# A pooling mixer and feed-forward trunk in split fp32: VectorE's transposes of three pairs of rows move within the second half's w_in products

## The chip, the cores and the metric

The kernel runs on one core of a Trainium2 chip. The metric is device time in microseconds (us): the median of three runs before the change is 1633.23 us (1632.07 to 1633.6).

The engines that matter here: TensorE (PE in the profile; PEld is its weight load), VectorE (DVE), ScalarE (ACT), GpSimd (POOL) and the queues from which transfers are issued (SPq, ACTq, and POOL's own).

## The reference, cut to what matters

Shapes: 2048 tokens of 1024 features, 16 meta tokens ahead of them, one layer (DEPTH is 1, so the mixer is the pooling one), d_ff is 2816.

```python
h = concatenate([meta, x])                       # 2064 x 1024
u = h @ a_w_in                                   # four groups of 256 columns
for g, w in enumerate((2, 4, 8, 16)):            # trailing mean over w tokens
    pooled[g] = (cs[hi, g] - cs[lo, g]) / (hi - lo)
y = einsum('btgc,gce->btge', pooled - u, a_w_group)
m = (y * a_scale) @ a_w_out
h = layer_norm(ALPHA * h + m, ln_mix_g, ln_mix_b)
gate, up = split(h @ ffn_w_gu, 2)
h = layer_norm(ALPHA * h + (silu(gate) * up) @ ffn_w_down, ln_ffn_g, ln_ffn_b)
return h[N_META:]
```

## The kernel before, in words

**Arithmetic.** Every fp32 operand of a product is split into a high part (a cast, on ScalarE, in functions that end in `_hi`) and a low part (original minus high, on VectorE, `_lo`). A product is then three matmuls of 128x512. The large products are done with seven block products instead of eight (sums and differences of quarter matrices, made on POOL and VectorE).

**Tiling.** The tokens are four blocks of 512 (b = 0 to 3), and two blocks are a half (h = 0, 1). For each half, `mixer_block(h)` computes u = x @ w_in in eight steps p, and `mixer_products(h)` the seven products with the folded group and output weights. The steps go through `STEPS = ((0,0), (0,1), (1,0), (1,1), (0,2), (0,3), (1,2), (1,3))`: block e of the half and chunk i of w_in, 256 columns. Step p is 48 matmuls on TensorE. The windows of the chunks are 16, 4, 8 and 2 (chunk 0 to 3). I call the eight steps of the second half p0 to p7.

**What a step brings with it.** When step p's matmuls are done, ScalarE copies them from PSUM to `stage` (`stage_u`, L1343). VectorE then pools them (`pool`, L1705 to L1720): copies of the 16 tokens of history, running sums (four, two, three or none), and a last subtraction into a `d` tile. TensorE has two PSUM places for the steps and takes the third step only when the first has been staged: step p waits for `stage_u` of step p-2. There is one `stage` tile, so `stage_u` of a step waits for the pooling of the step before it (`d_ready`). A chunk of w_in is used by two steps and is split anew in each half (`split_hi` L1308, `split_lo` L1672) into one of two places: the third chunk's split is needed by p4, the fourth's by p5. Its place comes free when p2, or p3, is done.

**The pairs.** During the second half's eight steps the normalised rows of the first half are transposed for the feed-forward product. They come back from DRAM in four pairs of row tiles, pi = 0 to 3. For each pair VectorE does four transposes (`turn_pair`, L1871), ScalarE scales and shifts them in eight instructions and issues their store (`scale_turned`, L1333 and L1323), and POOL makes four sums and issues their store (`pair_sums`, L987, L936, L994). The tiles of pairs 0 and 2 are `st_mix0`, those of pairs 1 and 3 `st_mix1`. The memory of `st_mix0` is also the tile `d12`, into which p4 and p5 are pooled. So the pooling of p4 in the second half waits for the store of pair 2 to land (`st_stored[0]` at 32) and for POOL's sums of pairs 0 to 2 (`ss_made` at 12). POOL's sums of a pair wait for its scaling; the transposes of pair 2 or 3 wait for the store of the pair that held the tile, and for its sums.

**Order.** Each engine runs its own instructions in the order in which the functions for it are written; nothing reorders them. The sync queue's order is written out too; its loads of the next x rows (`load_z`) wait for the number of transposes done (`turn_done`).

Of the kernel before, what the change touches and what calls it, by code (L numbers as in the profile page):

```python
# [31 lines left out]
def trunk(nc, x, x_t, meta_t, w_in, first_t, second_t, w_group_t, w_out, mix_g, mix_b, w_gu, w_down, ffn_g, ffn_b,  # L32
# [7 lines left out]
    TT = TOK // P  # L40
# [22 lines left out]
    def c_in(h, i):  # L63
        return MIX0 + h * HALF_CHUNKS + i
# [10 lines left out]
    def used_up(c):  # L75

        h, r = (c - MIX0) // HALF_CHUNKS, (c - MIX0) % HALF_CHUNKS
        return c + 1 if c < MIX0 else in_done(2 * h + 1, r) if r < PAIRS else mix_done(h, r - PAIRS)
# [13 lines left out]
    with ExitStack() as ctx:  # L92
# [256 lines left out]
        def raw_of(c, slot):  # L349
            return raw_first[:] if c == c_in(0, 0) else raw[:, slot]  # L350
# [58 lines left out]
        def st_of(pi):  # L409
            return st_mix[pi % 2] if pi < 4 else st_gu  # L410
# [893 lines left out]
        def _(act):  # L1304
            def split_hi(c, slot, kn=CHUNK):
                act.wait_ge(raw_landed[slot], (c - slot) * 8 - 8 * (GROUPS - 2))
                act.wait_ge(chunk_done, used_up(c - 2))
                nc.scalar.copy(split[:, slot, 0, 0:kn], raw_of(c, slot)[:, 0:kn]).then_inc(w_hi_ready, 1)  # L1308
# [12 lines left out]
            def store_turned(pi):  # L1321
                act.wait_ge(turn_taken, 2 * TT * (pi + 1))
                nc.scalar.dma_start(pair_forms(pi)[:, 0:3, :], st_of(pi)[:, 1:4].rearrange("p f k t -> p f (k t)")  # L1323
                                    ).then_inc(st_stored[pi % 2], 16)

            def scale_turned(pi, kh):

                act.wait_ge(turn_done, TT * pi + 3 + kh)
                if pi == 0:
                    act.wait_ge(mix_gb_kept, 1)  # L1330
                for k in range(KC):
                    both, kk = st_of(pi)[:, 2 * kh:2 * kh + 2, k, :], kh * KC + k
                    nc.scalar.activation(both, both, ACT.Identity, bias=mix_b_sb[:, kk:kk + 1],  # L1333
                                         scale=mix_g_sb[:, kk:kk + 1]).then_inc(turn_taken, 1)
                if kh:
                    store_turned(pi)

            def stage_u(b, i):
                act.wait_ge(chunk_done, in_done(b, i))
                if b or i:  # L1340

                    act.wait_ge(d_ready, staged_by(b, i) - 1)
                nc.scalar.mul(staged(), pair(i % 2), 1.0 / WINDOWS[ORDER[i]]).then_inc(u_staged, 1)  # L1343

            def d_hi(h, t):
                form_ready(act, h, t)

                act.wait_ge(chunk_done, in_done(2 * h, PAIRS - 1) if t < 2 else mix_done(h, t - 2))
                nc.scalar.copy(ring[h][t % 2][:, 0], FORM_D[t][:]).then_inc(d_hi_ready, 1)
# [58 lines left out]
            def stage_meta(i):  # L1408
                act.wait_ge(meta_rows_done, i + 1)
                if i >= 1:  # L1410
                    act.wait_ge(meta_u_done, i)
                nc.scalar.mul(meta_rows[:], acc[:, 4, 0:CW], 1.0 / WINDOWS[ORDER[i]]
                              ).then_inc(meta_rows_staged, 1)
# [43 lines left out]
            def norm(s, j):  # L1457
                act.wait_ge(shift_ready, s + 1)
                zz = zm[s % 2][:, j, :]
                nc.scalar.activation(zz, zz, ACT.Identity, bias=shift[:, j:j + 1],  # L1460
                                     scale=rstd[:, j:j + 1]).then_inc(normed, 1)

            def mixer_block(h):
                for p, (e, i) in enumerate(STEPS):
                    b = 2 * h + e
                    c = c_in(h, 0) + {0: 1, 3: 2, 4: 3, 7: 4}.get(p, 0)
                    if c > c_in(h, 0) and c != c_in(0, 1):
                        split_hi(c, c % 2)
                    if p >= 1:
                        stage_u(2 * h + STEPS[p - 1][0], STEPS[p - 1][1])  # L1470
                    if b == 0:
                        stage_meta(i)
                    if h and 2 <= p <= TT + 1:
                        scale_turned(p - 2, 0)
                        scale_turned(p - 2, 1)
                    if p >= 6:
                        d_hi(h, p - 6)
                    if p < 2:
                        x_hi(2 * h + 1, 2 * p)
                        x_hi(2 * h + 1, 2 * p + 1)  # L1480
                    if h and p == 0:
                        for j in range(TT):
                            norm(1, j)
# [185 lines left out]
        def _(dve):  # L1669
# [190 lines left out]
            def turn_pair(pi):  # L1860
                if pi < 2:

                    dve.wait_ge(d_lo_ready, NP)
                else:
                    dve.wait_ge(st_stored[pi % 2], 16 * (pi // 2))
                    dve.wait_ge(ss_made, 4 * (pi - 1))
                for step, n in enumerate(TURN_ORDER):
                    if step % 2 == 0:
                        dve.wait_ge(z_landed[1 - step // 2][pi], 16 + 16 * QT)
                    dst, src = turned_block(pi, n)  # L1870
                    nc.vector.transpose(dst, src).then_inc(turn_done, 1)  # L1871

            def mixer_block(h):
                for p, (e, i) in enumerate(STEPS):
                    c = c_in(h, 0) + {0: 1, 3: 2, 4: 3, 7: 4}.get(p, 0)
                    if c > c_in(h, 0) and c != c_in(0, 1):
                        split_lo(c, c % 2)
                    if p == 7:
                        d_sums(h, 0)
                        d_sums(h, 1)  # L1880
                    if h and p == 0:
                        rows_stats(0, 6)
                        stats_are_done(1)
                        aggregate(1)
                    if p < 2:
                        x_lo(2 * h + 1, 2 * p)
                        x_lo(2 * h + 1, 2 * p + 1)
                    if h == 0 and p in (1, 2, 5, 6):
                        taken = (1, 2, 5, 6).index(p)
                        take_meta(taken)  # L1890
                        dve.wait_ge(meta_u_taken, taken + 1)
                    if h == 0 and p == 1:
                        for n in range(2):
                            dve.wait_ge(fold_stored[n], 16 * GROUPS)
                    if h and p in (4, 5):
                        turn_pair(p - 2)
                    if p >= 1:
                        pool(2 * h + STEPS[p - 1][0], STEPS[p - 1][1])
                    if h and p in (1, 2):
                        turn_pair(p - 1)  # L1900
                    if p == 6:
                        d_lo(h, 0)

# [355 lines left out]
```

## Time and profile before

| What | Value |
|---|---|
| Median of the runs | 1633.23 us |
| Profiled execution, its own time | 1632.91 us |
| Its span (first to last instruction) | 1631.1 us |
| Granted TensorE clock over the span | 1.00 |
| PE busy | 1620.8 us, 99% |
| DVE, ACT, POOL busy | 65%, 37%, 39% |
| Transfers | 326.63 MB, 200 GB/s in the mean |

How to read it. An engine's busy time is a mean over stages that differ much. PE is busy almost throughout, so a change can matter only where it shortens or adds a wait of PE, and such waits are read one by one from the timeline. In a timeline row the first number is the start, the second the length of the group, and the bracket holds the idle time before it with what ended it. The releaser is inferred from semaphores.

### The profile page before, as it was taken

How to read it: one execution, taken by the hardware profiler on the slowest of the kernel's cores; microseconds unless marked ns; L12 is line 12 of the kernel's file. 1: busy time of each engine (PE TensorE's matmuls, PEld its weight loads, DVE VectorE, ACT ScalarE, POOL GpSimd, SP SyncE). 2: the span in 40 equal slices, each digit the busy share in tenths (PEclk: the TensorE clock that was granted, in tenths of full speed). 3: DMA queues.
4: the chain of work that ended last, by engine and by line, in shares of the span. 5: the costliest groups of instructions: out<-in, count | busy, mean ns of one | idle time of the engine just before them, and what ended most of it. 6: DMA issues, size and time to landing. Idle time of an engine off the chain costs nothing.

```text
span 1631.1 us, 18826 instructions
## 1 busy us (share of the span) xinstructions
PE 1620.8 (99%) x7169; PEld 1340.4 (82%) x7169; DVE 1052.5 (65%) x1111; ACT 608.1 (37%) x837; POOL 635.9 (39%) x440
## 2 busy tenths in 40 slices
PE   9999999999999999999999999999999999999998
PEld 7888887888888888888888888888888888888886
DVE  7758779998355556545756776676544443468866
ACT  6225454545434443434433333333333322222230
POOL 0420025025358667754456666666620000441000
PEclk9999999999999999999999999999999999999999
DMA  9563588444467666666856666665577544554542
GB/s 366 204 249 138 183 223 291 180 177 143 140 215 238 202 197 205 203 204 219 265 184 196 194 207 212 212 195 181 185 247 247 190 153 143 201 210 176 200 140 95
DMA packets 197001, 326.63 MB, mean 200 GB/s; under 512 B 8752, under 2 KB 140976, under 8 KB 188208
## 3 DMA queue, kind: packets, MB, share of 16 engines
q1 hardware_dynamic: 157216, 293.45, 53.9%
q10 hardware_dynamic: 37520, 23.60, 4.7%
q0 software_dynamic: 2176, 8.39, 1.4%
q8 instruction: 57, 0.93, 0.2%
q14 instruction: 32, 0.26, 0.0%
HBM read 223.16 MB, written 102.24 MB: 199 GB/s over the span
## 4 chain that ended last, share of the span: by engine, by line
PE 95%; DVE 2%; DMA 2%; issue 0%; ACT 0%; POOL 0%; SPq 0%; DVEq 0%; ACTq 0%
PE acc L1257 43%; PE acc L1287 19%; PE acc L1104 7%; PE turn L1257 7%; PE acc L1135 7%; PE turn L1287 6%; PE turn L1135 3%; PE acc L1167 1%; DVE sums L1717 1%; DMA dwr<-w_down 1%; DVE st_mix L1871 1%; DMA h_dram<-zm 1%; PE acc L1180 0%; DMA zm<-h_dram 0%; DVE split L1672 0%
## 5 line engine op out<-in xcount | busy, mean ns | idle before, releaser
L1257 PE MATMUL acc<-fa,wf 128*128 128x512 f32 x1584 | 362.8, 389 | 0.0
L1257 PE MATMUL acc<-fb,wf 128*128 128x512 f32 x1584 | 362.8, 389 | 0.0
L1257 PEld LDWEIGHTS acc<-fa,wf 128*128 128x128 f32 x1584 | 297.2, 188 | 61.8
L1257 PEld LDWEIGHTS acc<-fb,wf 128*128 128x128 f32 x1584 | 297.2, 188 | 61.8 <-issue 0.2
L1287 PE MATMUL acc<-dw,da 128*128 128x512 f32 x1386 | 315.6, 389 | 0.3 <-DVE dw L1972 0.3
L1287 PEld LDWEIGHTS acc<-dw,da 128*128 128x128 f32 x1386 | 260.1, 188 | 54.7 <-DVE dw L1972 0.7
L1857 DVE TENSOR_TENSOR wf<-wt,wf 128x512 fp32r<-128x512 f32 x132 | 130.1, 988 | 144.0 <-ACT wf L1454 144.0
L1857 DVE TENSOR_TENSOR wf<-wr,wf 128x512 fp32r<-128x512 f32 x176 | 181.8, 1039 | 38.8 <-ACT wf L1454 38.4
L936 POOL TENSOR_TENSOR wt<-wr,wt 128x512 f32<-128x512 f32 x88 | 138.7, 1577 | 154.6 <-DVE wf L1857 154.5
L1454 ACT CAST wf<-wr 128x512 fp32r<-128x512 f32 x176 | 108.7, 618 | 215.9 <-PE acc L1257 213.2
L1104 PE MATMUL acc<-mov,split 128*128 128x512 f32 x768 | 176.2, 390 | 1.8 <-DVE split L1672 1.8
L1966 DVE TENSOR_TENSOR da<-dar,da 128x1408 fp32r<-128x1408 f32 x56 | 92.1, 1644 | 132.0 <-ACT da L1555 132.0
L1104 PEld LDWEIGHTS acc<-mov,split 128*128 128x128 f32 x768 | 143.6, 188 | 32.2 <-issue 2.6
L1555 ACT CAST da<-dar 128x1408 fp32r<-128x1408 f32 x56 | 76.9, 1373 | 197.0 <-PE acc L1287 156.6
L1135 PE MATMUL acc<-split,ring 128*128 128x512 f32 x480 | 110.4, 389 | 0.0
L1287 PE MATMUL turn<-dw,da 128*128 128x512 f32 x462 | 105.9, 389 | 0.0
L1135 PEld LDWEIGHTS acc<-split,ring 128*128 128x128 f32 x480 | 90.1, 188 | 18.7
L1454 ACT CAST wf<-wt 128x512 fp32r<-128x512 f32 x132 | 81.9, 621 | 56.5 <-PE acc L1257 41.6
L1287 PEld LDWEIGHTS turn<-dw,da 128*128 128x128 f32 x462 | 86.7, 188 | 18.0
L936 POOL TENSOR_TENSOR wt<-wr 128x512 f32<-128x512 f32 x44 | 59.6, 1355 | 103.2 <-DMA wr<-w_gu 73.2
L1079 POOL TENSOR_TENSOR z<-z,z 128x512 f32<-128x512 f32 x8 | 12.2, 1526 | 199.1 <-DVE z L2106 199.1
L1972 DVE TENSOR_TENSOR dw<-dwr,dw 128x512 fp32r<-128x512 f32 x77 | 54.4, 732 | 41.5 <-ACT dw L1561 41.4
(151 smaller groups left out, 1810.8 us busy)
## 6 DMA issues: line engine op xcount, KB each, us to landing
wr<-w_gu SPq DMA_DIRECT2D x44, 1024.0 KB, 5.2
dar<-af_dram SPq DMA_DIRECT2D x56, 704.0 KB, 4.4
af_dram<-g ACTq DMA_DIRECT2D x32, 512.0 KB, 5.5
fs<-hf_dram SPq DMA_DIRECT2D x14, 1024.0 KB, 5.6
dt_raw<-w_down SPq DMA_DIRECT2D x22, 512.0 KB, 5.5
wt_dram<-dt_t SPq DMA_DIRECT2D x22, 512.0 KB, 3.5
sa<-af_dram SPq DMA_DIRECT2D x22, 512.0 KB, 8.2
af_dram<-sx SPq DMA_DIRECT2D x22, 512.0 KB, 4.7
```

Of the source, the lines that this page charges most:

```text
L936: return nc.gpsimd.tensor_tensor(out_, a, b, ALU.subtract)
L1104: mm = nc.tensor.matmul(acc[:, 2 * banks + m, :], w[:, a, k, m * P:(m + 1) * P], x_of[:, k, v, :], start=k == 0 and n3 == 0, stop=k == KT ...
L1135: mm = nc.tensor.matmul(bank_, ring[h][t % 2][:, v, k, m * P:(m + 1) * P], w[:, a, k, :], start=t in (0, 3) and k == 0 and n3 == 0, stop=k ...
L1167: mm = nc.tensor.matmul(acc[:, 2 * (q % 3) + n, :], gt[:, a, e, ct * P:(ct + 1) * P], w[:, v, e, n * TOK:(n + 1) * TOK], start=e == 0 and ...
L1257: mm = nc.tensor.matmul(dst, wf[:, slot, a, k, :], fa[half][i][:, v, :, k, :], start=i < 2 and k == 0 and n3 == 0, stop=k == KC - 1 and n3 ...
L1287: mm = nc.tensor.matmul(down_bank(k), da[k % 3][:, v, p, :], dw[:, slot, a, :], start=t < NP - 1 and p == 0 and n3 == 0, stop=p == JF - 1 ...
L1454: nc.scalar.copy(wf[:, (NP * n + i) % 8, 0].rearrange("p k n -> p (k n)"), w_source(n, i)).then_inc(wf_hi, 1)
L1555: nc.scalar.copy(da[k % 3][:, 0], dar[:, k % 2]).then_inc(da_hi, 1)
L1717: linked(nc.vector.tensor_tensor(nxt[:, :, lo:], cur[:, :, lo:], cur[:, :, lo - shift:H + TOK - shift], ALU.add))
L1857: nc.vector.tensor_tensor(wf[:, s, 1].rearrange("p k n -> p (k n)"), w_source(n, i), f32(wf[:, s, 0]).rearrange("p k n -> p (k n)"), ALU.s ...
L1966: nc.vector.tensor_tensor(da[k % 3][:, 1], dar[:, k % 2], f32(da[k % 3][:, 0]), ALU.subtract).then_inc(da_lo, 1)
L1972: nc.vector.tensor_tensor(dw[:, v % 16, 1, :], dwr[:, w % 2, v % JF % 2, :], f32(dw[:, v % 16, 0, :]), ALU.subtract).then_inc(dw_lo, 1)
```

## The change: three pairs' transposes take other places

The transposes, scalings and stores themselves are the same, and so is every wait. What moves, in the second half only:

- On VectorE the second pair (pi = 1) goes from behind p1's pooling, ahead of the third chunk's split, to behind the fourth chunk's split. The third pair (pi = 2) goes from there to a place behind p3's pooling, and is followed by the fourth (pi = 3), which stood there already.
- On ScalarE the first pair's scaling goes from ahead of the third chunk's cast to behind it, the second pair's from behind the staging of p2 to behind that of p3, and the third's from there to behind the staging of p4, ahead of the fourth pair's.

```diff
 # ScalarE, mixer_block(h), step p
                     if c > c_in(h, 0) and c != c_in(0, 1):
                         split_hi(c, c % 2)
+                    if h and p == 3:
+                        scale_turned(0, 0)
+                        scale_turned(0, 1)
                     if p >= 1:
                         stage_u(2 * h + STEPS[p - 1][0], STEPS[p - 1][1])
                     if b == 0:
                         stage_meta(i)
-                    if h and 2 <= p <= TT + 1:
-                        scale_turned(p - 2, 0)
-                        scale_turned(p - 2, 1)
+                    for pi in {4: (1,), 5: (2, 3)}.get(p, ()) if h else ():
+                        scale_turned(pi, 0)
+                        scale_turned(pi, 1)
 # VectorE, mixer_block(h), step p
-                    if h and p in (4, 5):
-                        turn_pair(p - 2)
+                    for pi in {4: (1,), 5: (2, 3)}.get(p, ()) if h else ():
+                        turn_pair(pi)
                     if p >= 1:
                         pool(2 * h + STEPS[p - 1][0], STEPS[p - 1][1])
-                    if h and p in (1, 2):
-                        turn_pair(p - 1)
+                    if h and p == 1:
+                        turn_pair(0)
```

On VectorE before, from the end of p1's pooling to the fourth chunk's split (`st_mix1_82` is the second pair's tile, `zm0`, `zm1` the rows that came back, `split` the two splits of w_in's third and fourth chunk, and between them stands p2's pooling with its four `sums`):

```order
L1720 SCALAR_TENSOR_TENSOR d0_60<-stage_73,sums0_68 128x1024
L1871 STREAM_TRANSPOSE st_mix1_82<-zm1_78 128x4x4x32 x2
L1871 STREAM_TRANSPOSE st_mix1_82<-zm0_77 128x4x4x32 x2
L1672 TENSOR_TENSOR split_70<-raw_71,split_70 128x2048
L1705 COPY stage_73<-hist_74 128x2x16
L1706 COPY hist_74<-stage_73 128x32
L1717 TENSOR_TENSOR sums1_69<-stage_73 128x2x526
L1717 TENSOR_TENSOR sums0_68<-sums1_69 128x2x524
L1717 TENSOR_TENSOR sums1_69<-sums0_68 128x2x520
L1717 TENSOR_TENSOR sums0_68<-sums1_69 128x2x512
L1720 SCALAR_TENSOR_TENSOR d1_61<-stage_73,sums0_68 128x1024
L1672 TENSOR_TENSOR split_70<-raw_71,split_70 128x2048
```

The same stretch of VectorE now (line numbers are three higher):

```order
L1723 SCALAR_TENSOR_TENSOR d0_60<-stage_73,sums0_68 128x1024
L1675 TENSOR_TENSOR split_70<-raw_71,split_70 128x2048
L1708 COPY stage_73<-hist_74 128x2x16
L1709 COPY hist_74<-stage_73 128x32
L1720 TENSOR_TENSOR sums1_69<-stage_73 128x2x526
L1720 TENSOR_TENSOR sums0_68<-sums1_69 128x2x524
L1720 TENSOR_TENSOR sums1_69<-sums0_68 128x2x520
L1720 TENSOR_TENSOR sums0_68<-sums1_69 128x2x512
L1723 SCALAR_TENSOR_TENSOR d1_61<-stage_73,sums0_68 128x1024
L1675 TENSOR_TENSOR split_70<-raw_71,split_70 128x2048
L1874 STREAM_TRANSPOSE st_mix1_82<-zm1_78 128x4x4x32 x2
L1874 STREAM_TRANSPOSE st_mix1_82<-zm0_77 128x4x4x32 x2
```

The second pair's transposes moved from ahead of the third chunk's split to behind the fourth's, past p2's pooling.

On VectorE before, what follows, up to the first copy of p4's pooling (`st_mix0_81` is the third pair's tile, `st_mix1_82` now the fourth's, and the pooling between them is p3's):

```order
L1871 STREAM_TRANSPOSE st_mix0_81<-zm1_78 128x4x4x32 x2
L1871 STREAM_TRANSPOSE st_mix0_81<-zm0_77 128x4x4x32 x2
L1705 COPY stage_73<-hist_74 128x2x16
L1706 COPY hist_74<-stage_73 128x32
L1717 TENSOR_TENSOR sums1_69<-stage_73 128x2x514
L1717 TENSOR_TENSOR sums0_68<-sums1_69 128x2x512
L1720 SCALAR_TENSOR_TENSOR d1_61<-stage_73,sums0_68 128x1024
L1871 STREAM_TRANSPOSE st_mix1_82<-zm1_78 128x4x4x32 x2
L1871 STREAM_TRANSPOSE st_mix1_82<-zm0_77 128x4x4x32 x2
L1705 COPY stage_73<-hist_74 128x2x16
```

And now, behind the second pair:

```order
L1708 COPY stage_73<-hist_74 128x2x16
L1709 COPY hist_74<-stage_73 128x32
L1720 TENSOR_TENSOR sums1_69<-stage_73 128x2x514
L1720 TENSOR_TENSOR sums0_68<-sums1_69 128x2x512
L1723 SCALAR_TENSOR_TENSOR d1_61<-stage_73,sums0_68 128x1024
L1874 STREAM_TRANSPOSE st_mix0_81<-zm1_78 128x4x4x32 x2
L1874 STREAM_TRANSPOSE st_mix0_81<-zm0_77 128x4x4x32 x2
L1874 STREAM_TRANSPOSE st_mix1_82<-zm1_78 128x4x4x32 x2
L1874 STREAM_TRANSPOSE st_mix1_82<-zm0_77 128x4x4x32 x2
L1708 COPY stage_73<-hist_74 128x2x16
```

The third pair moved behind p3's pooling and stands directly ahead of the fourth, and both ahead of p4's pooling.

On ScalarE before, from the staging of p1 to that of p4 (`split` is the cast of the third and of the fourth chunk, the `ACTIVATE` rows with x8 the scaling of the first, second and third pair, `hf_dram` their stores):

```order
L1343 ACTIVATE stage_73<-acc 128x2x512
L1333 ACTIVATE st_mix0_81<-st_mix0_81,mix_gb_sb 128x2x128 x8
L1323 DMA hf_dram<-st_mix0_81 128x3x512
L1308 CAST split_70<-raw_71 128x2048
L1343 ACTIVATE stage_73<-acc 128x2x512
L1333 ACTIVATE st_mix1_82<-st_mix1_82,mix_gb_sb 128x2x128 x8
L1323 DMA hf_dram<-st_mix1_82 128x3x512
L1308 CAST split_70<-raw_71 128x2048
L1343 ACTIVATE stage_73<-acc 128x2x512
L1333 ACTIVATE st_mix0_81<-st_mix0_81,mix_gb_sb 128x2x128 x8
L1323 DMA hf_dram<-st_mix0_81 128x3x512
L1343 ACTIVATE stage_73<-acc 128x2x512
```

And now:

```order
L1343 ACTIVATE stage_73<-acc 128x2x512
L1308 CAST split_70<-raw_71 128x2048
L1333 ACTIVATE st_mix0_81<-st_mix0_81,mix_gb_sb 128x2x128 x8
L1323 DMA hf_dram<-st_mix0_81 128x3x512
L1343 ACTIVATE stage_73<-acc 128x2x512
L1308 CAST split_70<-raw_71 128x2048
L1343 ACTIVATE stage_73<-acc 128x2x512
L1333 ACTIVATE st_mix1_82<-st_mix1_82,mix_gb_sb 128x2x128 x8
L1323 DMA hf_dram<-st_mix1_82 128x3x512
L1343 ACTIVATE stage_73<-acc 128x2x512
L1333 ACTIVATE st_mix0_81<-st_mix0_81,mix_gb_sb 128x2x128 x8
L1323 DMA hf_dram<-st_mix0_81 128x3x512
```

The cast of each chunk stands ahead of a scaling that it stood behind, the staging of p2 stays behind the first pair's, and those of p3 and p4 come ahead of the second and the third pair's. The fourth pair's scaling follows the third's.

## Rows read from the trace of the kernel before

**Rows 1.** The page's head: span, and busy time of TensorE.

```profile
span 1631.1 us, 18826 instructions
PE 1620.8 (99%) x7169; PEld 1340.4 (82%) x7169; DVE 1052.5 (65%) x1111; ACT 608.1 (37%) x837; POOL 635.9 (39%) x440
```

**Rows 2.** Timeline of TensorE around the second half's w_in steps.

```profile
201.62 43.68 PE L1104 MATMUL acc<-mov,split 128*128 128x512 f32 x192
245.46 11.16 PE L1104 MATMUL acc<-mov,split 128*128 128x512 f32 x48 [0.16 <-DVE split L1672]
258.26 32.95 PE L1104 MATMUL acc<-mov,split 128*128 128x512 f32 x144 [1.64 <-DVE split L1672]
291.05 5.60 PE L1135 MATMUL acc<-split,ring 128*128 128x512 f32 x24
```

**Rows 3.** Chain that ended last, by time: start, us, what.

```profile
255.83 2.30 DVE split L1672
...
291.21 5.44 PE acc L1135 x24
```

**Rows 4.** Timeline of VectorE, p0's pooling to p5's.

```profile
220.59 0.17 DVE L1705 COPY stage<-hist 128x32 f32<-128x32 f32 x1
...
222.18 3.79 DVE L1717 TENSOR_TENSOR sums<-sums 128x1048 f32<-128x1048 f32 x3
226.00 1.23 DVE L1720 SCALAR_TENSOR_TENSOR d<-stage,sums 128x1024 f32<-128x1024 f32 x1
...
238.03 4.37 DVE L1871 STREAM_TRANSPOSE st_mix<-zm 128x512 f32<-128x512 f32 x4
242.34 2.98 DVE L1672 TENSOR_TENSOR split<-raw,split 128x2048 fp32r<-128x2048 f32 x1
245.24 0.17 DVE L1705 COPY stage<-hist 128x32 f32<-128x32 f32 x1
...
247.95 6.70 DVE L1717 TENSOR_TENSOR sums<-sums 128x1048 f32<-128x1048 f32 x3
...
258.03 4.36 DVE L1871 STREAM_TRANSPOSE st_mix<-zm 128x512 f32<-128x512 f32 x4
262.30 0.15 DVE L1705 COPY stage<-hist 128x32 f32<-128x32 f32 x1
...
266.23 4.35 DVE L1871 STREAM_TRANSPOSE st_mix<-zm 128x512 f32<-128x512 f32 x4
271.49 0.18 DVE L1705 COPY stage<-hist 128x32 f32<-128x32 f32 x1 [0.91 <-POOL ss_mix L936]
...
276.57 2.19 DVE L1720 SCALAR_TENSOR_TENSOR d<-stage,sums 128x1024 f32<-128x1024 f32 x1
```

**Rows 5.** Timeline of ScalarE: a chunk's cast, the third pair's scaling, p5's staging.

```profile
237.74 1.92 ACT L1308 CAST split<-raw 128x2048 fp32r<-128x2048 f32 x1 [0.51 <-ACT st_mix L1333]
...
261.37 4.06 ACT L1333 ACTIVATE st_mix<-st_mix,mix_gb_sb 128x256 f32<-128x256 f32 x8 [4.33 <-DVE st_mix L1871]
...
278.86 1.03 ACT L1343 ACTIVATE stage<-acc 128x1024 f32<-128x1024 f32 x1 [5.25 <-DVE d L1720]
```

**Rows 6.** Timeline of POOL: the first of the third pair's four sums.

```profile
265.51 1.97 POOL L987 TENSOR_TENSOR ss_mix<-st_mix 128x512 f32<-128x512 f32 x1 [10.75 <-ACT st_mix L1333]
```

**Rows 7.** View of tile st_mix, 264 to 268 us: the third pair's store.

```profile
DMA to landing us min/median/max: 5.3/5.3/5.3
```

**Rows 8.** View of tile st_mix, 272 to 277 us: the fourth pair's store.

```profile
DMA to landing us min/median/max: 11.8/11.8/11.8
```

**Rows 9.** DMA view, 279 to 282 us: packets, MB, share (q0 POOL's, q1 SP's, q10 ACT's).

```profile
q0 software_dynamic: 128, 0.52, 42.4%
q1 hardware_dynamic: 129, 0.46, 37.7%
q10 hardware_dynamic: 128, 0.26, 22.4%
```

**Rows 10.** Timeline of TensorE at the program's start.

```profile
1.32 3.94 PE L1143 MATMUL turn<-idle 128*128 128x512 f32 x9 [1.32 <-POOL idle L1035]
```

## The prediction, on record before the result

> **What bounds the kernel now.** I read the page's head first: TensorE is busy for 99% of the span [rows 1], so only what lengthens or shortens a wait of TensorE can move the time. Next I read TensorE's timeline over the second half's eight w_in steps, p0 to p7, where the moved work lies [rows 2]. A group of 24 matmuls at full pace takes 5.44 us [rows 3], so a step of 48 takes 10.88. From p0's start at 201.62 the free grid of starts is p4 245.14, p5 256.02, p6 266.90, p7 277.78 and the end 288.66. The trace has p4 at 245.46 and p5 at 258.26, each released by VectorE's split of a w_in chunk, and the next stage at 291.05 [rows 2]. Of the 2.39 us behind the grid, 0.32 fall before p4, another 1.92 before p5 (1.64 shown as idle) and 0.15 after it. Counted back from 291.05, p7 started at 280.17. The chain of waits runs over VectorE's split at 255.83 [rows 3] and, from p5 on, over TensorE alone.
>
> VectorE's timeline says why the split was late: it is full [rows 4]. The transposes of the second pair (4.37 us at 238.03) stand ahead of the third chunk's split, and p2's pooling runs from 245.24 to 255.83, 10.6 us, where p0's with the same instructions takes 6.6 (220.59 to 227.23). Its sums beside POOL's take about 2.2 us each (6.70 for three) against 1.26 (3.79 for three).
>
> One more wait has almost no room. `stage_u` of p5 ran from 278.86 to 279.89 [rows 5], 0.28 us ahead of p7, which needs it. It stood behind p4's pooling, which began at 271.49 and ended at 278.76, and this began when POOL's sums of the third pair were done [rows 4]. The moved work acts on exactly this chain.
>
> **Part by part: what comes earlier.** The third chunk's cast no longer stands behind a scaling. It starts when p2 is done (201.62 + 3 x 10.88, about 234.4) and ends at 236.3. The first pair's scaling follows (4.06 us, the third pair's row [rows 5]) to 240.4, its store is issued, and p2's staging (1.03) ends at 242.0. VectorE splits the third chunk behind p1's pooling, from 238.0 to 240.3 (2.29, without the collision that made it 2.98 [rows 3, 4]), so p4 starts on the grid. Then VectorE idles for 1.7 us, as p2 isn't staged before 242.0. POOL's sums of the first pair now start at 240.5, and three of the four run beside p2's pooling. I charge each with the 1.0 us that the rows show: 6.6 + 3.0, ending at 251.5. The fourth chunk's split ends at 253.8, and p5 can start on the grid, at 256.02. Both waits on splits go: 2.24 us.
>
> **What comes later.** Behind that split come the second pair's transposes (4.3 us, to 258.1), then p3's pooling (4.0, as from 262.30 to 266.23 [rows 4], now to 262.0), and only then the third pair's. They start at 262.0 instead of 258.03, 4 us later although everything ahead of them was earlier: a pooling of 4.0 us was put in front, 1.7 us of idle was added, and less contention gave some back. Scaling ends 7.4 us after the transposes start (258.03 to 265.43 [rows 4, 5]), so at 269.4, and there the store is issued. POOL's four sums were done 13.3 us after the start (at 271.4, as p4's pooling shows [rows 4]); their first one took 1.97 beside VectorE's sums [rows 6], and is now free (1.3 like the others), so 12.7 and 274.7.
>
> p4's pooling waits for both the sums and the landing of this store. Before, the store landed 5.3 us after issue [rows 7], just inside the sums. Now it has company: the second pair's sums end on POOL at about 267, and their 1 MB store follows at once; the fourth pair's transposes (from 267.1, when the second pair's sums free the tile, to 271.4) release five loads of rows. The fourth pair's store of before lay in just such company and took 11.8 us [rows 8]. I take the middle of 5.3 and 11.8, 8.6 us, and land at 278.0. The bounds are 274.7 and 281.2.
>
> The rows show how the queues share: in 3 us with all three at work each moved 128 or 129 packets, and ScalarE's, with the smallest ones, 0.26 MB of them [rows 9]. The Trainium skill (DMA: Bandwidth & Descriptors, Queues, rings and completion order) says that each engine takes turns between the queues by packets, and the trace agrees. By that rule alone, with the 0.79 MB (128 x 3 x 512 words) at 0.087 MB per us throughout, the landing would take 9.1 us; with the first part beside one other queue it comes to about my 8.6.
>
> p4's pooling took 7.3 us beside POOL's sums of the fourth pair [rows 4]. It meets them again (POOL waits for its own second-pair store, which lands in the same crowd), so 278.1 + 7.3 = 285.4. Bounds: 5.3 without POOL (two sums and the end at their free 1.26 instead of 2.2), 8.3 if all four long instructions meet it. Staging p5 adds 0.1 + 1.03: 286.6. p7 starts there instead of 280.17. **Term one: +6.4 us**, in which the 2.24 gained are already used up, because p7 waits for staging and not for p6.
>
> **The clock behind the wait.** TensorE then idles from 277.78 to 286.6, 8.8 us. This trace has no such idle in its middle: the granted clock stands at 1.00 (the 2.4 GHz level) everywhere. The nearest row is the program's start: behind the pause before it, nine matmuls of the same 128x512 shape take 3.94 us, 0.438 each [rows 10], against 0.227 at full pace, although the clock column says 1.00 there too. That is the pace of the lower level. If the pause at p7 does the same, nine matmuls cost 9 x 0.211 = 1.9 us. Bounds: 0, and 3.2 if it is 15 matmuls. **Term two: +1.9 us**. The Trainium skill (TensorE: Matmul & The Clock Gate, Part 1) says that TensorE falls to 1.2 GHz when idle and regains 2.4 GHz only after activity; by it term two is in the sum, by the clock column of the start it isn't.
>
> **What costs nothing.** Transposes, scalings, sums and stores keep their number and size. The sync queue's loads of the next rows wait for transposes: two of them and a chunk load behind them come about 4 us later (the chunk is cast only after p6), the other five about 0.8. The fourth pair's scaling, now behind the third's, ends at about 274.5, while p4's pooling is held anyway. Behind p5's staging VectorE's work moves with TensorE's, both by 7 to 8 us, so the room between them stays. The end is untouched.
>
> **Sum.** 1632.91 (the profiled execution) + 6.4 + 1.9 = 1641.2. The median of the runs is 0.3 above that execution, so 1641.5.
>
> **Rivals.**
> - Late landing, but the clock holds: 1641.5 - 1.9 = 1639.6. For it: the clock column of rows 10 never leaves 1.00. Against it: the pace there.
> - The store lands inside the sums. Then p4's pooling starts at 274.8 and p7 at 274.8 + 7.3 + 1.1 = 283.2: +3.0, with the clock term 1638.1, without it 1636.2; if it also misses POOL's sums, +1.0 and 1634.2. For it: 5.3 us last time. Against it: 1 MB more in flight.
> - Not slower: VectorE's relief is all that counts. The two split waits go, p7 starts at 277.78, and the time is 1633.2 - 2.4 = 1630.8. It decides where p5 is staged by 277.8, so p4's pooling must start by 277.8 - 1.1 - 5.3 = 271.4, earlier than before; even a tie needs a start by 273.8. The third pair's transposes would have to start at 258.7 (for 271.4 behind 12.7), 3.3 us ahead of my 262.0. For it: VectorE does gain before p5. Against it: no row among the six in front can shrink by that.
> - Worse in two places: p2's pooling meets all of POOL's sums and more, the fourth chunk's split misses 256.02 as well, and all later terms grow; with the upper bounds 290.7 for p7, +10.5 + 3.2, 1646.9.
>
> That the change does nothing is out: the order of both engines moves as shown.
>
> **How the numbers follow.** Late landing with the lower clock 0.45 (1641.5), late landing without it 0.23 (1639.6), landing inside the sums with the clock term 0.12 (1638.1), the same without it 0.09 (1634.2 to 1636.2), relief alone 0.04 (1630.8), worse 0.07 (up to 1646.9). About 0.2%, 3.3 us, is what can be told from no change, so slower means above 1636.5: 0.45 + 0.23 + 0.12 + 0.07 = 0.87. Relief alone gives 2.4 us, which is within that bound too; I keep 0.01 of its 0.04 for more. So within is 0.09 + 0.03 = 0.12 and faster 0.01. The range 1635.5 to 1645.0 leaves out the case of relief, part of the within case and the worst end.
>
> **What would show it.** Right: no wait of TensorE on a split at p4 and p5; VectorE idle for 1 to 2 us ahead of p2's pooling; the third pair's transposes at about 262; p4's pooling released at 275 to 281 by the third pair's store or sums; one wait of TensorE of 6 to 10 us for p5's staging; slower matmuls right behind it. Wrong: p7 at or before 280.2, the third pair's transposes before 259, a PE wait on a split that stays, or waits in the mixer's products that were not there.

## The result, and the profile after

| | Before | After |
|---|---|---|
| Median, us | 1633.19 (1632.07 to 1633.6) | 1646.51 (1646.1 to 1646.95) |
| Ratio to before | | 1.0084 (95% interval 1.0071 to 1.0096) |
| Span of the profiled execution, us | 1631.1 | 1645.0 |
| Mean granted clock | 1.00 | 0.994 |

The change makes the kernel 13.3 us slower. The forecast was slower, at 1641.5 us with a range up to 1645.0; the measured time lies above the range.

TensorE's timeline after, where [rows 2] stand for before:

```profile
201.47 76.32 PE L1104 MATMUL acc<-mov,split 128*128 128x512 f32 x336
291.77 13.94 PE L1104 MATMUL acc<-mov,split 128*128 128x512 f32 x48 [13.97 <-ACT stage L1343]
305.55 5.60 PE L1135 MATMUL acc<-split,ring 128*128 128x512 f32 x24
```

The 336 matmuls are p0 to p6 in one piece: both waits on splits are gone. Then comes one wait of 14 us, for `stage_u` of p5, and p7 takes 13.8 us (291.77 to 305.55) instead of 10.9. Counted from p0's start, p7 comes 11.75 us later than before (90.30 against 280.17 - 201.62 = 78.55), and its slow pace adds 2.90. Those 14.65 us, less 0.15 by which p0 itself starts earlier and 0.6 by which the stretch from p7's end to the span's end is shorter, are the 13.9 between the spans.

VectorE's timeline after; the first row is the second pair's transposes, the next two are the third's and the fourth's, and the rest is p4's pooling:

```profile
253.60 4.27 DVE L1874 STREAM_TRANSPOSE st_mix<-zm 128x512 f32<-128x512 f32 x4
...
261.72 4.32 DVE L1874 STREAM_TRANSPOSE st_mix<-zm 128x512 f32<-128x512 f32 x4
266.94 4.32 DVE L1874 STREAM_TRANSPOSE st_mix<-zm 128x512 f32<-128x512 f32 x4 [0.90 <-issue]
282.48 1.90 DVE L1708 COPY stage<-hist 128x32 f32<-128x32 f32 x1 [11.22 <-DMA hf_dram<-st_mix]
284.41 0.18 DVE L1709 COPY hist<-stage 128x32 f32<-128x32 f32 x1
284.51 2.30 DVE L1720 TENSOR_TENSOR sums<-stage 128x1036 f32<-128x1036 f32 x1
...
289.37 1.23 DVE L1723 SCALAR_TENSOR_TENSOR d<-stage,sums 128x1024 f32<-128x1024 f32 x1
```

The third pair starts at 261.72 (forecast 262.0). p4's pooling starts at 282.48 (forecast 278.1), released by a transfer, and takes 8.1 us (forecast 7.3). Its first copy, of 32 elements in a row, takes 1.90 us against 0.18 before.

The chain of waits after names the transfer (start, us, what):

```profile
265.03 4.07 ACT st_mix L1333 x8
269.10 0.02 issue
269.12 13.28 DMA hf_dram<-st_mix
...
290.69 1.03 ACT stage L1343
291.72 0.04 issue
291.77 13.94 PE acc L1104 x48
```

The third pair's store takes 13.28 us, where it took 5.3 [rows 7]. The clock fell behind the wait; columns are the stretch, its length, PE busy, granted clock, share and rate of the transfers:

```profile
280.00:284.00 4.00, 0.00 (x0) 0.58 1.04 418
284.00:291.00 7.00, 0.00 (x0) 0.50 0.55 222
292.00:296.00 4.00, 4.00 (x10) 0.50 0.63 240
296.00:298.00 2.00, 2.00 (x6) 0.58 0.00 0
298.00:300.00 2.00, 2.00 (x10) 1.00 0.43 78
```

From about 281 to 297.5 us the granted clock is 0.50, the 1.2 GHz level.

### The profile page after: what moved, and what is told of

It reads as the page before. It is cut to its first block, busy times and chain, and to the rows that moved or that the text cites. A ratio compares the mean times of both kernels' runs of the same rounds, so it can differ in the third digit from the quotient of the medians.

```text
span 1645.0 us, 18826 instructions
## 1 busy us (share of the span) xinstructions
PE 1622.6 (99%) x7169; PEld 1342.6 (82%) x7169; DVE 1053.7 (64%) x1111; ACT 607.9 (37%) x837; POOL 630.5 (38%) x440
## 4 chain that ended last, share of the span: by engine, by line
PE 96%; DVE 2%; DMA 1%; ACT 1%; issue 0%; POOL 0%; DVEq 0%; ACTq 0%; SPq 0%
PE acc L1257 44%; PE acc L1287 19%; PE acc L1104 8%; PE turn L1257 7%; PE acc L1135 7%; PE turn L1287 6%; PE turn L1135 3%; PE acc L1167 1%; DMA hf_dram<-st_mix 1%; ACT st_mix L1333 1%; DVE sums L1720 1%; PE acc L1180 0%; DVE st_mix L1874 0%; DMA raw<-w_out 0%; DVE stage L1708 0%
```

## The experiments

Theory: the time went into the third pair, transposed later, whose store p4's pooling waits for, and into the lower clock behind that wait. Which transfers made the store late, and what made the pooling long, was open after the first four runs. The runs were made on three chips, so each is set against before on its own chip.

| Run | Median, us | Before on the same chip | Ratio, 95% interval |
|---|---|---|---|
| e1_third_back | 1638.14 (1635.57 to 1639.94) | 1632.51 | 1.0034 (1.0022 to 1.0045) |
| e2_second_back | 1641.69 | 1632.51 | 1.0058 (1.0043 to 1.0073) |
| e3_fill | 1644.66 | 1632.51 | 1.0075 (1.0058 to 1.0092) |
| e4_second_mid | 1634.33 | 1632.51 | 1.0011 (1.0002 to 1.0021) |
| e5_rows_late | 1646.03 | 1632.91 | 1.0080 (1.0065 to 1.0095) |
| e6_sums_store_late | 1638.24 | 1632.91 | 1.0033 (1.0021 to 1.0045) |
| e7_after_hold | 1643.25 | 1632.91 | 1.0062 (1.0045 to 1.0079) |
| e8_second_back_hold | 1634.85 | 1632.91 | 1.0011 (1.0002 to 1.0020) |
| e9_mid_hold | 1630.22 | 1632.85 | 0.9985 (0.9976 to 0.9994) |
| e10_before_hold | 1630.90 | 1632.85 | 0.9988 (0.9979 to 0.9997) |

### One part undone: the third pair back ahead of p3's pooling (e1)

The edit against the changed kernel, the same on ScalarE and VectorE (cut to the part that differs):

```diff
-{4: (1,), 5: (2, 3)}
+{4: (1, 2), 5: (3,)}
```

> The changed kernel with one part undone: the third pair stands again ahead of p3's pooling, now directly behind the second pair; the fourth alone in front of p4's pooling. Theory (the time went into the late third pair, whose store p4's pooling waits for, and into the lower clock behind that wait): transposes of the third pair start at 258, its store is issued at about 265.6 with only a chunk load beside it and lands in 5 to 6 us, POOL's sums of it end at about 273 behind those of the second pair; p7 starts at 280 to 282.5, a wait of TensorE of 2 to 5 us, 1633 to 1638 us. Rival A (the second pair's late place is what costs): the time stays at 1645 or more. Rival B (it is the number of transposes in a row ahead of a pooling that costs, wherever they stand): a wait of TensorE for p3's pooling appears at p6, and the time is above 1638.

1638.14 us, just above the theory's range, and the reason is another: rival B's. TensorE's timeline:

```profile
254.71 12.18 PE L1104 MATMUL acc<-mov,split 128*128 128x512 f32 x53
270.31 23.85 PE L1104 MATMUL acc<-mov,split 128*128 128x512 f32 x96 [3.42 <-ACT stage L1343]
```

The wait stands ahead of p6, not p7. p3's pooling behind two pairs of transposes ran from 262.0 to 269.1 beside POOL's sums, 7.1 us instead of 4.0, so p4 was staged late. The third pair's store landed in 6.7 us, as the theory said, and was not the bound. The clock fell behind this wait too (0.60 from 270 to 272 us, 0.54 from 272 to 274): p6 and p7 take 23.7 us (270.31 to 294.00) instead of 21.8. Wait and clock together are 5.3 of the 5.6 us above before. Putting the third pair back wins 8 of the 13 us, but directly behind the second pair it makes p6 late.

### The other part undone: the second pair back (e2)

The edit on VectorE, against the changed kernel. On ScalarE the scalings of the first and of the second pair go back to where they were before.

```diff
-                    for pi in {4: (1,), 5: (2, 3)}.get(p, ()) if h else ():
+                    for pi in {5: (2, 3)}.get(p, ()) if h else ():
                         turn_pair(pi)
...
-                    if h and p == 1:
-                        turn_pair(0)
+                    if h and p in (1, 2):
+                        turn_pair(p - 1)
```

> The other part undone: the second pair is transposed and scaled where it was before the change (behind p1's pooling), only the third pair moves behind p3's pooling, ahead of the fourth. Theory: the wait on the split at p5 comes back (1.6 us), the third pair's transposes start at about 262.2, its store shares the queues with the five row loads but not with a store of the second pair's sums, and lands 8 to 11 us after its issue at 269.6; p7 starts at 286 to 289 instead of 280.2, the clock falls to 0.5 behind the wait and costs 2.9 us more: 1641 to 1645 us. Rival A (the second pair's move, by its sums' store in flight, is what made the store late): the landing takes 5 to 6 us, p4's pooling waits for the sums, p7 at 283, 1636 to 1639 us. Rival C (the third pair's place costs nothing by itself): 1633 us.

1641.69 us, inside the theory's range, but not by its mechanism. The store landed in 5.7 us, as rival A expected, although the five row loads were in flight (issued from 270.43 on, the store at 269.24):

```profile
DMA to landing us min/median/max: 5.7/5.7/5.7
```

VectorE's timeline shows where the time went instead:

```profile
274.99 4.51 DVE L1705 COPY stage<-hist 128x32 f32<-128x32 f32 x1 [4.63 <-DMA hf_dram<-st_mix]
279.52 0.18 DVE L1706 COPY hist<-stage 128x32 f32<-128x32 f32 x1
279.62 2.32 DVE L1717 TENSOR_TENSOR sums<-stage 128x1036 f32<-128x1036 f32 x1
```

A copy of 128x32 took 4.51 us. With it p4's pooling took 10.7 us, and TensorE waited 6.7 us ahead of p7. POOL's rows beside it, the fourth pair's sums:

```profile
274.87 0.78 POOL L994 DMA_DIRECT2D hf_dram<-ss_mix  x1 [0.40 <-POOL ss_mix L936]
275.66 1.30 POOL L987 TENSOR_TENSOR ss_mix<-st_mix 128x512 f32<-128x512 f32 x1
276.91 1.29 POOL L936 TENSOR_TENSOR ss_mix<-st_mix 128x512 f32<-128x512 f32 x1
278.16 1.28 POOL L936 TENSOR_TENSOR ss_mix<-ss_mix,st_mix 128x512 f32<-128x512 f32 x1
279.52 1.32 POOL L936 TENSOR_TENSOR ss_mix<-st_mix,ss_mix 128x512 f32<-128x512 f32 x1
```

POOL runs at its free pace of 1.3 us each, and the copy ends in the gap between its third and fourth instruction. This run gave two new suspects: the store of the second pair's sums, for the landing, and POOL's instructions, for the pooling.

### Matmuls in the wait (e3)

```diff
+            FILL = 56
...
+                    if h and p == 7:
+                        chunk_is_split(c_in(h, i))
+                        wx = split[:, c_in(h, i) % 2].rearrange("p s (k n) -> p s k n", n=CW)
+                        for _ in range(FILL):
+                            nc.tensor.matmul(turn[:, 1, :], wx[:, 0, 0, 0:P], mov_of(b)[:, 0, 0, :], start=True, stop=True)
                     if p >= 2:
                         pe.wait_ge(u_staged, 2 * PAIRS * h + p - 1)
```

> The changed kernel with 56 more matmuls of 128x512 on TensorE between p6 and the wait of p7; they write a PSUM place that nothing reads, and take 12.7 us of the 14 us wait. Theory (the clock fell because TensorE was idle): granted clock 1.00 throughout, p7's 48 matmuls take 10.9 us instead of 13.8, p7 starts where it started, time 1643.6 us. Rival D (the slow matmuls behind the wait come from something else, as from the transfers or VectorE's and POOL's traffic): p7 keeps 13.8 us and the time stays at 1646.5.

TensorE's timeline:

```profile
278.06 12.86 PE L1213 MATMUL turn<-mov,split 128*128 128x512 f32 x56
292.17 8.02 PE L1105 MATMUL acc<-mov,split 128*128 128x512 f32 x34 [1.26 <-ACT stage L1349]
```

The granted clock is 1.00 in every stretch up to 304 us, and p7 takes 11.0 us (292.17 to 303.20) instead of 13.8, starting as long after p0 as in the changed kernel (90.27 against 90.30). The transfers and VectorE's and POOL's work beside p7 were still there, so rival D falls: the idle caused the slow matmuls, and the clock's share is 2.75 us by the traces. The medians show less, 1.9 us across two chips (1644.66, where 1643.6 was expected), with intervals that overlap.

### The second pair into VectorE's idle time (e4)

The edit on VectorE, against the kernel before:

```diff
-                    if h and p in (4, 5):
+                    if h and p in (3, 4, 5):
                         turn_pair(p - 2)
...
-                    if h and p in (1, 2):
-                        turn_pair(p - 1)
+                    if h and p == 1:
+                        turn_pair(0)
```

ScalarE casts the third chunk ahead of the first pair's scaling, as in the changed kernel.

> The kernel before with the second pair between the third chunk's split and p2's pooling, where VectorE idled for 1.2 us in the changed kernel; ScalarE's third-chunk cast ahead of the first pair's scaling as in the changed kernel; third and fourth pair as before the change. Theory: the third chunk's split is early (240.5), the second pair ends at 244.8, p2's pooling at about 253, the fourth chunk's split at about 255.5, in front of the grid's 256.0; the third pair starts at about 256 and its store and sums are done by 270, p7 on the grid at 277.8: no wait of TensorE over 0.5 us between p0 and p7, 1631 us. Rival E (POOL's sums of two pairs beside p2's pooling slow it past the split's due time): a wait on the split at p5 of 1 to 2 us remains, 1632 to 1633 us.

1634.33 us: my theory missed, and rival E's wait came, larger than it said.

```profile
258.39 34.48 PE L1104 MATMUL acc<-mov,split 128*128 128x512 f32 x144 [2.38 <-DVE split L1675]
```

The third chunk's split was early, but p2's pooling ran from 244.24 to 254.9 (10.7 us) and the split behind it took 3.38 us instead of 2.29, both beside POOL's sums of the second pair (247.50 to 256.1). Counted from p0, p5 starts only 0.3 us later than before (56.94 against 56.64), which is not the 1.8 us between the medians. The rest is the clock, which this wait of 2.4 us took down:

```profile
258.00:260.00 2.00, 1.61 (x4) 0.65 1.02 387
260.00:262.00 2.00, 2.00 (x6) 0.50 0.29 111
```

p5 to p7 take 34.3 us (258.39 to 292.71), where they took 32.8 before. The one wait of 2.4 us cost more than before's two delays of 0.3 and 1.9 us (0.16 and 1.64 us of them idle), behind which the clock stayed at 1.00. The move gained nothing while POOL was left to collide.

### Which transfer made the store late (e5, e6)

The five row loads behind `load_mix(1, 2)`:

```diff
+            load_mix(1, 2)
             load_z(2, 3)
             for j in range(TT):
                 load_z(3, j)
-            load_mix(1, 2)
```

> The changed kernel with the sync queue's last five loads of the next rows issued behind the load of the third product's weights (about 298 us) instead of ahead of it (271 to 275 us). Theory F (the third pair's store is late because of what is in flight with it): only the store of the second pair's sums shares the queues with it, the store lands 8 to 9 us after its issue at 269.1 instead of 13.3, p4's pooling starts at 277 to 278, p7 at 286 to 287.5, time 1641 to 1643 us. Rival G (the five row loads take nothing from it): landing stays above 12 us, 1646 us.

The store of the second pair's sums behind the third pair's sums:

```diff
 def pair_sums(pi):
...
+    if pi == 2:
+        store_sums(1)
+    if pi != 1:
+        store_sums(pi)
```

> The changed kernel with POOL issuing the store of the second pair's sums behind the arithmetic of the third pair's sums (274.4 us) instead of ahead of it (267.3 us). Theory F: the third pair's store then has no such company, as in the run in which the second pair kept its old place, where it landed in 5.7 us; it lands at about 275. POOL is then held ahead of its second store until the first has landed, so that its fourth pair's sums don't meet p4's pooling: pooling 275 to 280.5, p7 at 281.5, a wait of 3.7 us, and 1 to 3 us more by the lower clock: 1635 to 1638 us. Rival G' (the row loads alone make the store late): landing over 10 us, 1643 us or more.

Landing of the third pair's store, first with the row loads late, then with the sums' store late:

```profile
DMA to landing us min/median/max: 10.2/10.2/10.2
```

```profile
DMA to landing us min/median/max: 7.0/7.0/7.0
```

Each takes something off the 13.3: the row loads 3.1 us, the sums' store 6.3. Rival G falls by the landing (10.2 us, and it said above 12), but theory F's 8 to 9 us was missed too. The time with the row loads late is 1646.03 us, the number that G gave, and my theory's 1641 to 1643 missed. VectorE's timeline in that run says why:

```profile
279.43 3.91 DVE L1708 COPY stage<-hist 128x32 f32<-128x32 f32 x1 [8.10 <-DMA hf_dram<-st_mix]
...
288.33 1.22 DVE L1723 SCALAR_TENSOR_TENSOR d<-stage,sums 128x1024 f32<-128x1024 f32 x1
```

The pooling starts 3.1 us earlier and takes 10.1 us instead of 8.1, because POOL's sums of the fourth pair (from 279.59) now begin together with it; p7 still waits 12.8 us. Counted from p0, p7 starts 1.2 us earlier than in the changed kernel and then takes 13.3 us instead of 13.8. This gain is still there when the feed-forward's last product starts (1218.03 against 1219.54). By 1264 us the lead has shrunk to 0.45 us, in part by a wait of 0.73 us for VectorE at 1225.72 that the changed kernel's trace hasn't. So the number that G gave came about by other steps than G's. Why the lead was lost there is open. With the sums' store late POOL was held elsewhere:

```profile
276.13 0.18 DVE L1715 COPY stage<-hist 128x32 f32<-128x32 f32 x1 [4.88 <-DMA hf_dram<-st_mix]
...
280.24 1.23 DVE L1730 SCALAR_TENSOR_TENSOR d<-stage,sums 128x1024 f32<-128x1024 f32 x1
```

The pooling takes 5.3 us, p7 waits 4.78 us, the clock falls to 0.50 nevertheless, p7 takes 13.05 us, and the median is 1638.24, just above what was expected.

### POOL held until the pooling is done (e7, e8)

`d_ready` stands at 13 when p4's pooling is done, and at 11, which the next section uses, when p2's is.

```diff
+            HELD = {3: 13}
 def pair_sums(pi):
...
+    if pi in HELD:
+        pool.wait_ge(d_ready, HELD[pi])
```

On the changed kernel:

> The changed kernel with POOL's sums of the fourth pair waiting until p4's pooling is done (one wait on d_ready more). Theory H (POOL's instructions block VectorE's small history copy and its sums one by one): p4's pooling takes 5.3 to 5.5 us instead of 8.1 from 282.5, p7 starts at 289.0, 2.7 us less: 1643.8 us. Rival I (the long copy waits for something else, as the landing of the last parts of the store): the first copy keeps 1.9 us and the time falls by 1 us at most.

```profile
282.16 0.18 DVE L1712 COPY stage<-hist 128x32 f32<-128x32 f32 x1 [10.65 <-DMA hf_dram<-st_mix]
...
286.26 1.22 DVE L1727 SCALAR_TENSOR_TENSOR d<-stage,sums 128x1024 f32<-128x1024 f32 x1
```

On the kernel with the second pair back:

> The kernel with the second pair in its old place and the third behind p3's pooling, and the same hold of POOL: sums of the fourth pair only when p4's pooling is done. Without the hold this pooling ran from 275.0 to 285.7, of which 4.5 us are one 128x32 copy. Theory H: 275.0 to 280.4, p7 at 281.5, a wait of TensorE of 1.5 us, too short for the clock to fall: 1633.5 to 1636 us instead of 1641.7. Rival I: the copy still takes over 3 us, since it waits for the store, and the time stays above 1640.

```profile
275.81 0.18 DVE L1709 COPY stage<-hist 128x32 f32<-128x32 f32 x1 [4.52 <-DMA hf_dram<-st_mix]
...
279.92 1.23 DVE L1724 SCALAR_TENSOR_TENSOR d<-stage,sums 128x1024 f32<-128x1024 f32 x1
```

Theory H holds twice. The copy is back at 0.18 us and the pooling at 5.3, with the store landing nearly as without the hold (12.7 us against 13.3, and 5.6 against 5.7). The changed kernel comes down to 1643.25 and the other from 1641.69 to 1634.85 us. There TensorE's wait at p7 is 1.18 us, those on splits at p4 and p5 are 0.90 and 1.63, and the clock stays at 1.00.

### A version that beats both (e9, e10)

The same hold for the second pair's sums too (`HELD = {1: 11, 3: 13}`), on the kernel of e4 and on the kernel before:

> The kernel of the fourth experiment (second pair between the third chunk's split and p2's pooling) with POOL held: the second pair's sums start only when p2's pooling is done, the fourth pair's only when p4's is. Theory H (POOL's sums beside VectorE's pooling made the split of the fourth chunk late): p2's pooling takes 6.6 us (244.3 to 250.9), the split ends at 253.2, ahead of the grid's 256.0; p7 on the grid at 277.8; no wait of TensorE over 0.3 us from p0 to p7; 2.2 to 2.5 us less than before. Rival J (POOL's sums then come too late for what follows, and a wait of the same size shows up at p7 or behind): no change, within 1 us of before.

> The kernel before with nothing but the same two holds of POOL. Theory H: p2's pooling takes 6.6 us (245.3 to 251.9), the fourth chunk's split ends at 254.2, ahead of 256.2; the wait at p4 (0.2 to 0.3 us) stays, those at p5 (1.9) and p7 (0.15) go: 2.0 us less than before. Rival J: the waits come back at p7 or behind, within 1 us of before.

VectorE in the first of the two, p2's pooling and the split behind it, and TensorE from p0 to p7:

```profile
247.20 3.79 DVE L1724 TENSOR_TENSOR sums<-sums 128x1048 f32<-128x1048 f32 x3
...
252.16 2.29 DVE L1679 TENSOR_TENSOR split<-raw,split 128x2048 fp32r<-128x2048 f32 x1
```

```profile
201.65 87.20 PE L1108 MATMUL acc<-mov,split 128*128 128x512 f32 x384
```

All 384 matmuls are one piece, and the next stage starts at 288.69 instead of 291.05. Measured: 1630.22 us, 2.6 less than before on that chip, and 1630.90, 1.95 less, with nothing but two waits on POOL added to the kernel before. There the wait at p4 stayed, at 0.70 us (expected 0.2 to 0.3). The intervals of the two against each other overlap.

## Why the prediction was wrong

By its own steps:

- **The direction and the chain were right.** The rows after show the waits on splits gone, VectorE idle ahead of p2's pooling (1.23 us), the second pair's transposes at 253.6, the third's at 261.7, the store issued at 269.1 (forecast 269.4), and p7 waiting for p5's staging. Two signs missed by size: p4's pooling was released at 282.48, not by 281, and the wait was 14 us, not 6 to 10.
- **What failed is the landing inside term one.** I took 8.6 us with 11.8 as the upper bound, and it was 13.3: 4.4 of the missing 5.2 us of term one. The middle of two rows was no estimate of how much was in flight. The upper row [rows 8] was for a store with the row loads and one store of sums; here there was the chunk load ahead of it as well, as there was ahead of the store of [rows 7]. e6 takes 6.3 us off by moving the sums' store, e5 takes 3.1 off by moving the row loads. Together that is 9.4, more than the 8.0 between 13.3 and the 5.3 of before, so the two effects overlap: in e2, without the sums' store, the row loads left the landing at 5.7. The prediction had the sums' store in the company; what it lacked was its price. Its second working, 0.79 MB at 0.087 MB per us, priced only the moving: ScalarE's queue moved 0.81 MB from 273 to 280 us, faster than that. What the working left out is the time with no packet at all, at least 3.9 us behind the issue at 269.12, and the last 2.4 us up to the landing at 282.4, when this queue had moved as many bytes as the store has.
- **p4's pooling took 8.1 us, not 7.3.** The bound of 8.3 held. I counted only the sums as slowed by POOL. The traces show that the 32-element copy can be held as well, 1.9 us here and 4.5 in e2. The trace of before had such a copy, in p5's pooling, which I passed over:

```profile
280.13 1.20 DVE L1706 COPY hist<-stage 128x32 f32<-128x32 f32 x1
```

e7, with POOL held, shows that the whole excess over 5.3 is POOL's.
- **Term two was 2.9 us, not 1.9.** The mechanism was right, as e3 shows, and the bound of 3.2 held. The nine matmuls at the start were too few; at the lower level p7 ran from 291.8 to about 297.5. The Trainium skill (TensorE: Matmul & The Clock Gate, Part 1) has an idle TensorE fall to 1.2 GHz, and the trace agrees: 0.50 from 281 us on. Of the single waits in these runs 1.2 and 1.6 us left the clock at 1.00, and 2.4, 3.4, 4.8, 6.7 and 14 us didn't. What the fall costs doesn't grow steadily with the wait: 1.5 us behind 2.4 (e4), 1.9 behind 3.4 (e1), 2.2 behind 4.8 (e6), 3.0 behind 6.7 (e2), 2.3 behind 10.6 (e7) and 2.9 behind 14.
- **p2's pooling took 9.7 us, as charged (9.5)**, from 241.8 to 251.5, and the fourth chunk's split was early. The number was right in part by luck: I charged three sums with 1.0 us each, and two of the three went into the two copies, 1.21 and 1.20 us long:

```profile
241.81 1.21 DVE L1708 COPY stage<-hist 128x32 f32<-128x32 f32 x1 [1.23 <-ACT stage L1343]
```

- **The range was too narrow.** The worst case, 1646.9 us, was in the text, was all but met, and had a chance of 0.07. It was met as a number, not as told: the fourth chunk's split was not late, and p7 started 1.1 us behind its bound of 290.7, which a smaller clock term and a shorter end made up. The landing passed its bound, and the other two terms came out in the upper half of theirs. I know of no common cause: in e5 the landing was 3.1 us earlier and the pooling 2.0 us longer, and the clock's loss doesn't follow the wait (above).

The step that failed is the landing time of the third pair's store, put at 8.6 us and measured at 13.3; it falls to 7.0 when POOL's store of the second pair's sums is out of its way. The clock's loss is a second term, a third too small.

## What to carry to other kernels

Before moving an instruction behind another on a full engine, follow its last consumer and look at what will be in flight then: a store's landing depends on its company more than on its size (5.3 to 13.3 us for the same 0.79 MB here). Where several uncertain terms follow each other on one path, add their bounds and keep that end inside the range; here the sum of the bounds was 1646.9, the range ended at 1645.0, and 1646.5 was measured. A single wait can also cost more than two shorter ones of nearly the same sum: in e4 the clock fell behind one of 2.4 us, and in the kernel before it stayed at 1.00 behind delays of 0.3 and 1.9. And where VectorE is full while POOL has time, hold POOL's work out of VectorE's way before reordering VectorE: two added waits gained 2 us where three moved pairs lost 13.

## What the runs showed of the hardware

- **One small copy can wait for several of POOL's instructions.** VectorE's 128x32 fp32 copy took 0.18 us alone, and 1.9, 3.9 and 4.5 us beside POOL's back-to-back sums, which kept their 1.3 us. VectorE's sums of two inputs took turns with POOL instead, about 2.2 us each against 1.26. The Trainium skill (SBUF — State Buffer, Who interferes with whom) has GpSimd share a pair of ports with VectorE's copies in their two-port modes, the one that comes first holding it for its whole instruction, and contend for the read side with instructions of two inputs. The trace agrees that the copy is blocked: it ends where one of POOL's instructions ends (in e2 at 279.50 and 279.44). In e2 it let three instructions pass, and in e5 its 3.9 us span three as well (POOL's from 279.59 to 283.3), while in p2's pooling each of two copies waited for one only, 1.2 us. Why it is one here and three there is open.
- **POOL issues its next store only when the one before has landed.** Its second store waited 5.5 us in the changed kernel, to 279.84, and 11.2 us in e6, to 286.27, in both named by the profile as released by its own earlier store. The kernel asks for no such wait at that place.

```profile
279.84 0.77 POOL L994 DMA_DIRECT2D hf_dram<-ss_mix  x1 [5.49 <-DMA hf_dram<-ss_mix]
```

Where the sums were done earlier, the other traces agree: before, a store issued at 271.77 landed 12.0 us later and the next went out at 284.10; in e2 the numbers are 274.87, 11.6 and 286.77. This decides when POOL's next sums start, and so whom they meet: it is how 2 of the 3 us that the landing gained in e5 went back into the pooling.
- **One queue can take most of the transfers for a while.** In the changed kernel, from 273 to 276 us and from 276 to 279, the queues moved

```profile
q0 software_dynamic: 196, 0.79, 65.2%
q10 hardware_dynamic: 123, 0.25, 21.5%
q1 hardware_dynamic: 42, 0.17, 13.9%
```

```profile
q1 hardware_dynamic: 205, 0.78, 63.2%
q10 hardware_dynamic: 204, 0.42, 35.7%
```

POOL's store of sums (q0), issued 1.9 us ahead of the third pair's (q10), took the largest share first. Why it got 196 packets to 123, while in [rows 9] all three had 128, is in part that q10 began late: from 270 to 273 us it had none, from 273 to 274 it had 17, while the chunk load (q1) and then q0 moved. In e6 and e2, without the sums' store, q10's first packets came from 271 to 272, for a store issued at the same time. So some 2 of e6's 6.3 us are an earlier start and the rest is pace. Once q0 was nearly done, SyncE's row loads (q1) and ScalarE's stores (q10) had the same number of packets, and the loads, with the larger ones, nearly twice the bytes. That fits e5. The fourth pair's store, issued on q10 at 274.32, moved some of its bytes before the third's had all landed: by 280 us q10 had moved 0.81 MB, and the third's 0.79 MB had landed only at 282.4. What that store costs the third's was not tested.
